# First stage by chunks with VectorE's low parts, down products one up tile later, 346 feed-forward columns

## The chip, the cores and the metric

The kernel runs on one core of one Trainium2 chip. The metric is the device time of one execution in microseconds; the kernel before took 2233.31 us (median of three runs, 2232.62 to 2235.86).

## What is computed

One inference step of a hybrid decoder layer. 1024 prompt tokens with 16 meta tokens ahead of them, and 8 single tokens of running sequences, go through a normalization, one wide projection (queries, keys, values, and the inputs and gates of a recurrent branch), attention beside the recurrence, an output projection, and then the feed-forward stage, which the change touches most. Cut to that part, for the prompt:

```python
n = rms_norm(x, g_mix)
q, k, v, xr, gr, gates = jnp.split(n @ w_in, SPLITS, axis=-1)
...
up, ffn_buf_new = causal_dwconv(rms_norm(x, g_ffn) @ w_up, ffn_buf, w_ffn_conv, b_ffn_conv)
ua, ub = jnp.split(up, 2, axis=-1)
x = x + (jax.nn.gelu(ua) * ub) @ w_down
...
y_prompt = rms_norm(xp, g_final)[:, META_TOKENS:]
```

The convolution has three taps and looks back two tokens. The model width is 1024, the inner width 2816 (each half of `up`). The rows of the 16 meta tokens are not part of `y_prompt`; their keys and values, and the last two rows of `up` for each sequence, are outputs.

## The kernel before

Activations lie with channels on the partitions and tokens along the columns: 8 decode tokens, 16 meta tokens, 1024 prompt tokens and 2 spare columns, 1050 in all, taken in three chunks of `CW` = 350. Every wide product is made of three fp32r matmuls: each operand is split into a rounded high part (an fp32r copy, made by ScalarE) and a low part (the difference, made by VectorE or GpSimd), and `project_part` (L83) issues high x high, high x low and low x high for each of the 8 blocks of 128 channels, 24 matmuls for one chunk of one 128-channel tile ("a piece").

There are five phases, each a block that all engines leave together. Within one, every engine runs its own list of instructions in the order written, and semaphores tie them together; DMAs are issued by SyncE, in order.

**`phase_qkv` (L92).** Nine token tiles (24 tokens, then eight of 128) are loaded, squared and summed by ScalarE (L279), scaled by VectorE (L343), transposed by TensorE into `a_xt` (L419), multiplied by the weight of the norm by VectorE (L356), rounded by ScalarE into `n_hi` (L298), and subtracted by GpSimd into `n_lo` (L260). Two weight tiles are rounded in between (L285) and subtracted by GpSimd (L254). TensorE waits for all nine low parts and then makes 12 pieces for keys and values (four channel tiles `j` times three chunks `c`, by `j` first), each emptied by ScalarE from one of two banks (L308) into `kv_ch`. Then it transposes these (L448), and projects the queries.

**`phase_mix`** (attention, recurrence, gates) is the longest and isn't touched. **`phase_out` (L1391)** projects, adds the residual, normalizes each token tile again (L1520 to L1539), and writes `n_hi` and `n_lo` for the next phase.

**`phase_ffn` (L1583).** The inner width is taken in 11 turns of two 128-channel pairs. A turn has four up tiles (two of each half, three pieces each, from the banks of `p_up` in alternation), each emptied by ScalarE (`up_tile`, L1720), run through the convolution by VectorE (`conv`, seven chained operations, L1787 to L1801), the first of each pair through a gelu on ScalarE (L1725), and multiplied (`gated`, L1807). The product is rounded by ScalarE (`high_a`, L1730) and subtracted by VectorE (`low_a`, L1814). The down products of a turn are 24 chunks of 6 matmuls (8 output tiles times three chunks, L1870) that VectorE adds into `y` (L1823) from four banks. They are issued during the next turn, six behind each of its four up tiles. Weights come through two raw slots of `w_raw`; ScalarE rounds them (`high_up` L1706, `high_down` L1711), GpSimd subtracts (`low_up` L1676, `low_down` L1681), and SyncE loads the next one as soon as the low part is made. The first turn's up tiles stand ahead of the loop, the last turn's down products behind it. The order written for ScalarE around a turn's boundary is:

```python
high_down(0, nth(m, DOWNC, DOWNC - 1), 1, 16 * nth(m, 3, 2))
high_down(1, nth(m, DOWNC, DOWNC - 1), 0, 16 * nth(m, 3, 3))
high_a(m, 0)
up_tile(i, 0, (0, 1))
high_a(m, 1)
high_up(1, nth(i, UPC, -1, 6), 1, 16 * nth(m, 3, 3))
up_tile(i, 0, (2,))
```

where a rounding of down weights waits for the previous turn's last down product. On TensorE it is, for `u` from 0 to 3, `up_tile(m + 1, u, ...)` and then `down(m, ..., down_part(u))`; on VectorE `add_down(m, down_part(u))`, then `conv(m + 1, u)`, and `gated` behind each second one, with `low_a(m)` ahead of it all.

**`phase_last` (L1898)** transposes `y` back, adds the residual, normalizes and stores.

## Time and profile before

| | |
|---|---|
| median of three runs | 2233.31 us |
| the profiled execution | 2233.16 us, span 2231.4 us |
| mean granted TensorE clock | 0.937 |
| TensorE matmul busy | 1941.0 us (87%), 14580 matmuls |
| VectorE / ScalarE / GpSimd busy | 1209.2 (54%) / 941.7 (42%) / 247.5 us (11%) |
| up products L87, 3 groups | 1056 matmuls of 350 columns each, 325 ns mean |
| down products L1870 in the loop, 3 groups | 480 matmuls of 350 columns each, 328 to 332 ns mean |
| loads of up weights, issue to landing | 512 KB each, 3.7 us |

A matmul's duration overlaps its neighbours', so starts and not durations give its pace. A row of a timeline gives the start in us from the span's start, the duration, engine, line, operation and tiles, and in brackets how long the engine stood idle before and whose result ended that. A GpSimd, VectorE or ScalarE row with "x2" merges two instructions that follow each other.

### The profile page before, as it was taken

The numbers are of one execution on the slowest core, as the hardware profiler recorded it, in microseconds if no ns is written. First come the engines' busy times: TensorE is split into PE (matmuls) and PEld (weight loads), VectorE is DVE, ScalarE is ACT, GpSimd is POOL, SyncE is SP. The second block draws the span as 40 slices with busy tenths as digits, with TensorE's granted clock in tenths as the row PEclk, the third lists the DMA queues.
The fourth block names the chain that finished last, engine by engine and source line by source line (L and its number), as shares of the span: only waits on it lengthen the run. The fifth ranks groups of instructions, "written<-read, shape, count | busy, mean of one in ns | idle before, by whom it ended". The sixth has DMA issues, their size and how long they took to land. (4 is left out here: it accounts for less than half of the span.)

```text
span 2231.4 us, 41433 instructions
## 1 busy us (share of the span) xinstructions
PE 1941.0 (87%) x14580; PEld 1764.3 (79%) x14580; DVE 1209.2 (54%) x2020; ACT 941.7 (42%) x1514; POOL 247.5 (11%) x117
## 2 busy tenths in 40 slices
PE   3997898979797988979797796899999999999985
PEld 3897887758585867768585586899999999999985
DVE  6100566647484756647485534555555455545555
ACT  4112577666666666666667211221221222212213
POOL 4111000000000000000001202211221122212210
PEclk9999998979898998979898898999999999999998
DMA  3242312131222222131222221101111111111104
GB/s 114 77 114 70 103 44 78 51 84 49 78 62 74 77 58 59 51 84 48 79 58 78 93 91 56 57 22 54 47 47 38 38 47 47 38 38 47 47 19 168
DMA packets 198746, 144.02 MB, mean 65 GB/s; under 512 B 58293, under 2 KB 187894, under 8 KB 198548
## 3 DMA queue, kind: packets, MB, share of 16 engines
q1 hardware_dynamic: 198574, 141.80, 21.8%
q8 instruction: 99, 1.62, 0.3%
q14 instruction: 73, 0.60, 0.1%
HBM read 124.38 MB, written 17.61 MB: 64 GB/s over the span
## 5 line engine op out<-in xcount | busy, mean ns | idle before, releaser
L87 PE MATMUL d_p_up<-n_hi,d_w_hi 128*128 128x350 f32 x1056 | 343.7, 325 | 14.0 <-POOL d_w_lo L1676 7.7
L87 PE MATMUL d_p_up<-n_lo,d_w_hi 128*128 128x350 f32 x1056 | 342.7, 325 | 0.0
L87 PE MATMUL d_p_up<-n_hi,d_w_lo 128*128 128x350 f32 x1056 | 342.5, 324 | 0.0
L1823 DVE TENSOR_TENSOR mix<-mix,d_p_down 128x350 f32<-128x350 f32 x264 | 137.2, 520 | 323.8 <-PE d_p_down L1870 323.8
L1720 ACT ACTIVATE d_up<-d_p_up 128x350 f32<-128x350 f32 x132 | 60.6, 461 | 502.3 <-PE d_p_up L87 502.3
L87 PE MATMUL b_p_proj<-n_hi,b_w_hi 128*128 128x350 f32 x768 | 268.0, 349 | 4.5 <-ACT r_gr L969 4.5
L87 PE MATMUL b_p_proj<-n_lo,b_w_hi 128*128 128x350 f32 x768 | 252.6, 329 | 0.0
L87 PE MATMUL b_p_proj<-n_hi,b_w_lo 128*128 128x350 f32 x768 | 251.9, 328 | 0.0
L87 PEld LDWEIGHTS d_p_up<-n_hi,d_w_hi 128*128 128x128 f32 x1056 | 200.6, 190 | 15.0 <-POOL d_w_lo L1676 8.1
L1072 DVE TENSOR_TENSOR_SCAN b_sums<-b_sums 128x720 f32<-128x720 f32 (+16 forms) x136 | 171.1, 1258 | 60.2 <-ACT b_sums L1006 55.1
L87 PEld LDWEIGHTS d_p_up<-n_hi,d_w_lo 128*128 128x128 f32 x1056 | 200.6, 190 | 0.0
L87 PEld LDWEIGHTS d_p_up<-n_lo,d_w_hi 128*128 128x128 f32 x1056 | 200.4, 190 | 0.0
L1233 PE MATMUL b_p_z<-b_k_in,b_q_in 64*64 64x360 f32 (+16 forms) x1024 | 101.9, 460 | 102.2 <-ACT b_z L954 46.5
L1870 PE MATMUL d_p_down<-d_a_hi,d_wd_hi 128*128 128x350 f32 x480 | 159.4, 332 | 23.8 <-DVE d_a_lo L1814 23.8
L953 ACT ACTIVATE b_sums<-b_p_z,b_bias 128x720 f32<-128x720 f32 (+16 forms) x136 | 94.8, 697 | 197.5 <-PE b_p_z L1240 145.1
L1676 POOL TENSOR_TENSOR d_w_lo<-w_raw,d_w_hi 128x1024 fp32r<-128x1024 f32 x45 | 114.2, 2549 | 522.1 <-ACT d_w_hi L1706 522.1
L1058 DVE COPY mix<-b_p_misc 128x64 f32 (+2 forms) x136 | 29.9, 220 | 248.9 <-PE b_p_misc L1271 241.1
L1870 PE MATMUL d_p_down<-d_a_hi,d_wd_lo 128*128 128x350 f32 x480 | 158.3, 330 | 0.0
L87 PEld LDWEIGHTS b_p_proj<-n_hi,b_w_hi 128*128 128x128 f32 x768 | 151.9, 198 | 7.5 <-ACT r_gr L969 6.4
L1870 PE MATMUL d_p_down<-d_a_lo,d_wd_hi 128*128 128x350 f32 x480 | 157.6, 328 | 0.0
L87 PEld LDWEIGHTS b_p_proj<-n_lo,b_w_hi 128*128 128x128 f32 x768 | 151.0, 197 | 0.0
L87 PEld LDWEIGHTS b_p_proj<-n_hi,b_w_lo 128*128 128x128 f32 x768 | 149.1, 194 | 0.0
(248 smaller groups left out, 3916.9 us busy)
## 6 DMA issues: line engine op xcount, KB each, us to landing
w_raw<-in_w_in SPq DMA_DIRECT2D x45, 512.0 KB, 4.8
w_raw<-in_w_up SPq DMA_DIRECT2D x45, 512.0 KB, 3.7
b_page<-in_cache_k SPq DMA_DIRECT2D x128, 128.0 KB, 2.1
b_page<-in_cache_v SPq DMA_DIRECT2D x128, 128.0 KB, 2.1
w_raw<-in_w_down SPq DMA_DIRECT2D x22, 512.0 KB, 3.2
b_q_in<-q_scr SPq DMA_DIRECT2D x272, 32.0 KB, 2.2
q_scr<-a_q_stage SPq DMA_DIRECT2D x16, 260.0 KB, 3.3
mix<-in_x_prompt SPq DMA_DIRECT2D x8, 512.0 KB, 7.3
```

The lines of the kernel that those rows point to most:

```text
L87: last = pe.matmul(out, w[:, k, :], x[:, k, col:col + CW], start=(k == 0 and w is w_hi and x is x_hi), stop=(k == KT - 1 and w is w_lo))
L953: own.mark(act.activation(so, pz, ACT.Abs, bias=bias[:, 0:1]))
L1058: dve.tensor_copy(g.mix[:, bass.ds(i if s >= 0 else i - 1, 1), FIRST + q0:FIRST + q0 + nq] .rearrange("p a c -> p (a c)"), p_av[:, 0:nq]). ...
L1072: dve.tensor_tensor_scan(pos[:, ::-1], so[:, ::-1], pos[:, ::-1], 0.0, ALU.add, ALU.add)\
L1233: last = pe.matmul(banks[bank][QB * a:QB * (a + 1), 0:k1 - k0], q_in[rows, Q_AT[s], a, :], k_in[rows, k0:k1], start=True, stop=k1 <= diagonal)
L1676: pool.tensor_tensor(w_lo[:, slot, :, :], w_raw[:, raw, :, :], w_hi[:, slot, :, :].bitcast(F32), ALU.subtract).then_inc(lo_ready, 1)
L1720: act.activation(up[:, u % 2, CW * c:CW * (c + 1)], p_up[:, n % 2, 0:CW], ACT.Copy).then_inc(up_out, 1)
L1823: dve.tensor_tensor(to, to, p_down[:, n % 4, 0:CW], ALU.add).then_inc(down_out, 1)
L1870: last = pe.matmul(p_down[:, n % 4, 0:CW], w[:, k, P * tile:P * (tile + 1)], a[:, k, CW * c:CW * (c + 1)], start=(k == 0 and w is wd_hi an ...
```

## The change

Five things. In the first stage the pieces are made in another order (`FIRST_PIECES`: chunk by chunk for the first two channel tiles, then tiles 2 and 3), the first two in halves between the transposes of token tiles 5 to 8; each waits only for the token tiles of its own chunk. VectorE makes the low parts of the token tiles and of the first two weights, in a loop that runs one tile behind the multiply; ScalarE squares two tiles ahead, and SyncE's order of loads follows. In the feed-forward loop no down product follows the first up tile of a turn and eight follow each of the other three; the weight of the second up tile is loaded, rounded and subtracted ahead of the two down weights, the second of which is rounded after the second chunk of the turn's first up tile is emptied. And the feed-forward stage leaves out 14 of the 16 meta tokens: the 8 decode tokens are moved to columns 14 to 21, next to the last two meta tokens that the convolution still needs, and the stage's chunks are 346 columns from column 12 on. The last stage reads the decode tokens from there and leaves out the meta tokens' rows. The convolution loses the memset that had set the columns ahead of the prompt to zero.

```diff
+FIRST_PIECES = [(j, c) for c in range(CHUNKS) for j in range(2)] + [(j, c) for j in (2, 3) for c in range(CHUNKS)]
...
                 for t in range(2, TILES):
                     load_x(t)
-                    if t == 4:
-                        load_w(0, 1, K_COL)
-                load_w(1, 2, K_COL + P)
+                    if t in (3, 5):
+                        load_w(t // 2 - 1, t // 2, K_COL + P * (t // 2 - 1))
...
-                    sp.wait_ge(proj_out, 2 + CHUNKS * (j + 1))
+                    sp.wait_ge(proj_out, 2 + FIRST_PIECES.index((j, CHUNKS - 1)) + 1)
...
-                for t in range(TILES):
-                    c0, nr = token_tile(t)
-                    pool.wait_ge(hi_ready, t + 1)
-                    pool.tensor_tensor(g.n_lo[:, :, c0:c0 + nr], tmp[:, t % 2, :, 0:nr],
-                                       g.n_hi[:, :, c0:c0 + nr].bitcast(F32), ALU.subtract).then_inc(lo_ready, 1)
-                    if t == TILES - 2:
-                        low_part(0, 1)
-                low_part(1, 2)
...
                 square(0)
+                square(1)
                 for t in range(TILES + 1):
...
-                    if t + 1 < TILES:
-                        square(t + 1)
+                    if t + 2 < TILES:
+                        square(t + 2)
...
-                    if t in (7, 9):
-                        high_part((t - 7) // 2, 3 * (t - 5) // 2, 16)
+                    if t in (5, 7):
+                        high_part((t - 5) // 2, 3 * (t - 3) // 2, 16)
+                    if t == TILES:
+                        kv_piece(0)
...
+                for p in range(2, len(FIRST_PIECES)):
+                    kv_piece(p)
+                    if p in (4, 5):
+                        high_part(p - 4, 6 + p + 1, 32)
...
+                    if t >= 2:
+                        u = t - 2
+                        c0, nr = token_tile(u)
+                        dve.wait_ge(hi_ready, u + 1)
+                        dve.tensor_tensor(g.n_lo[:, :, c0:c0 + nr], tmp[:, u % 2, :, 0:nr],
+                                          g.n_hi[:, :, c0:c0 + nr].bitcast(F32), ALU.subtract).then_inc(lo_ready, 1)
+                    if t in (5, 7):
+                        n = (t - 5) // 2
+                        dve.wait_ge(w_hi_ready, n + 1)
+                        dve.tensor_tensor(w_lo[:, n, :, :], w_raw[:, n, :, :], w_hi[:, n, :, :].bitcast(F32),
+                                          ALU.subtract).then_inc(w_lo_ready, 1)
...
+                def first_piece(p, k0, k1):
+                    j, c = FIRST_PIECES[p]
+                    if k0 == 0:
+                        pe.wait_ge(lo_ready, tiles_for_chunk(c))
+                        if c == CHUNKS - 1:
+                            pe.wait_ge(consts, 9)
+                        pe.wait_ge(w_lo_ready, j + 3)
+                        pe.wait_ge(proj_out, p + 1)
...
-                pe.wait_ge(lo_ready, TILES)
-                pe.wait_ge(consts, 9)
+                    if t in (5, 7):
+                        first_piece(t // 2 - 2, 0, KT // 2)
+                    if t in (6, 8):
+                        first_piece(t // 2 - 3, KT // 2, KT)
+                for p in range(2, 6):
+                    first_piece(p, 0, KT)
...
+FTOK = HEAD_ROWS - 2
+FDEC = FTOK - DEC
+F0 = FDEC - 2
+FW = (COLS - F0) // CHUNKS
...
-            return range(DOWNC // 4 * u, DOWNC // 4 * (u + 1))
+            return range(DOWNC // 3 * (u - 1), DOWNC // 3 * u) if u else range(0)
...
                 with sp.Fori(0, TURNS - 1, 1) as m:
-                    load_down(1, nth(m, 6, 5), m, 0)
-                    load_down(0, nth(m, 6, 6), m, 1)
-                    for n in (1, 2, 3):
+                    load_up(1, nth(m, 6, 5), m + 1, 1)
+                    load_down(0, nth(m, 6, 6), m, 0)
+                    load_down(1, nth(m, 6, 7), m, 1)
+                    for n in (2, 3):
                         load_up(n % 2, nth(m, 6, n + 6), m + 1, n)
...
-                    low_down(0, nth(m, 2, 0), 1)
-                    low_down(1, nth(m, 2, 1), 0)
-                    for n in (1, 2, 3):
+                    low_up(1, nth(m, 4, 5), 1)
+                    low_down(0, nth(m, 2, 0), 0)
+                    low_down(1, nth(m, 2, 1), 1)
+                    for n in (2, 3):
                         low_up(n % 2, nth(m, 4, n + 4), n % 2)
...
-                    high_down(0, nth(m, DOWNC, DOWNC - 1), 1, 16 * nth(m, 3, 2))
-                    high_down(1, nth(m, DOWNC, DOWNC - 1), 0, 16 * nth(m, 3, 3))
+                    high_up(1, nth(i, UPC, -1, 6), 1, 16 * nth(m, 3, 2))
+                    high_down(0, nth(m, DOWNC, DOWNC - 1), 0, 16 * nth(m, 3, 3))
                     high_a(m, 0)
-                    up_tile(i, 0, (0, 1))
+                    up_tile(i, 0, (0,))
                     high_a(m, 1)
-                    high_up(1, nth(i, UPC, -1, 6), 1, 16 * nth(m, 3, 3))
+                    up_tile(i, 0, (1,))
+                    high_down(1, nth(m, DOWNC, DOWNC - 1), 1, 16 * nth(m, 3, 3))
                     up_tile(i, 0, (2,))
...
-                        project(pe, p_up[:, n % 2, 0:CW], w_hi[:, u % 2], w_lo[:, u % 2],
-                                g.n_hi, g.n_lo, CW * c).then_inc(up_done, 1)
+                        project(pe, p_up[:, n % 2, 0:FW], w_hi[:, u % 2], w_lo[:, u % 2],
+                                g.n_hi, g.n_lo, F0 + FW * c, FW).then_inc(up_done, 1)
...
                     for u in range(4):
-                        up_tile(m + 1, u, nth(m, 6, 6 + u if u else 4, 2))
-                        down(m, nth(m, 6, 6, 2), down_part(u))
+                        up_tile(m + 1, u, nth(m, 6, (4, 5, 8, 9)[u], 2))
+                        down(m, nth(m, 6, 7, 2), down_part(u))
```

The other lines of the diff follow from the new column numbers: the bounds of the convolution, the gelu, the products and the additions, two more small memsets for the two spare columns 12 and 13, the head tile's multiply in `phase_out` in two parts (8 decode and 2 meta columns), and the head tile's rows in `phase_last`.

## Rows read from the trace of the kernel before

**Rows 1.** Busy us by engine in stretches; then granted clock, DMA share, GB/s

```profile
52.20:101.60 49.40, 48.54 (x289) 47.67 (x290) 4.82 (x18) 8.40 (x15) 9.51 (x5) 1.00 0.22 60
...
212.00:1366.00 1154.00, 971.33 (x8672) 810.52 (x8672) 692.15 (x1142) 700.49 (x1140) 27.04 (x15) 0.90 0.25 69
...
1438.90:2165.40 726.50, 692.85 (x4248) 690.03 (x4249) 394.51 (x682) 154.06 (x219) 150.29 (x60) 0.98 0.14 42
```

**Rows 2.** What TensorE waited for: total us, times, longest us

```profile
PE a_xt L419 <- DVE mix L343: 27.6, 8, 7.2
...
PE d_p_down L1870 <- DVE d_a_lo L1814: 23.8, 10, 2.5
...
PE d_p_up L87 <- ACT d_up L1720: 6.3, 2, 4.9
...
PE a_proj L87 <- POOL n_lo L260: 6.9, 1, 6.9
```

**Rows 3.** Timeline, first stage, VectorE: start, duration (us), instruction, [idle before]

```profile
12.31 0.79 DVE L343 TENSOR_SCALAR mix<-mix,a_stat 128x1024 f32<-128x1024 f32 x1
13.02 1.21 DVE L356 TENSOR_TENSOR a_tmp<-a_xt,par 128x1024 f32<-128x1024 f32 x1
...
15.64 2.48 DVE L343 TENSOR_SCALAR mix<-mix,a_stat 128x1024 f32<-128x1024 f32 x1
```

**Rows 4.** Timeline, first stage, ScalarE, GpSimd and TensorE

```profile
10.51 1.06 ACT L279 ACTIVATE a_junk<-mix 128x1024 f32<-128x1024 f32 x1 [2.98 <-DMA mix<-in_x_prompt]
...
15.40 2.18 POOL L260 TENSOR_TENSOR n_lo<-a_tmp,n_hi 128x1024 fp32r<-128x1024 f32 x1 [2.85 <-ACT n_hi L298]
...
52.27 0.66 PE L87 MATMUL a_proj<-n_hi,a_w_hi 128*128 128x350 f32 x1 [6.95 <-POOL n_lo L260]
...
101.59 1.05 PE L448 MATMUL a_xt<-ident,a_kv_ch 128*24 128x128 f32 x8 [0.55 <-ACT a_kv_ch L308]
```

**Rows 5.** Single lines' instructions, VectorE: min/median/max ns

```profile
L1539 DVE TENSOR_TENSOR n_lo<-r_rg,n_hi x9: 360/1226/1227, 1263.2 to 1361.0; 128x1024 fp32r<-128x1024 f32 x8, 128x192 fp32r<-128x192 f32 x1
...
L1038 DVE TENSOR_TENSOR b_w_lo<-w_raw,b_w_hi x33: 1215/1224/1226, 215.7 to 1178.6; 128x1024 fp32r<-128x1024 f32 x33
```

**Rows 6.** Timeline, TensorE: 55 intervals of 350 columns, 36 of 512

```profile
1501.96 0.32 PE L87 MATMUL d_p_up<-n_hi,d_w_hi 128*128 128x350 f32 x1
...
1510.80 0.32 PE L87 MATMUL d_p_up<-n_lo,d_w_hi 128*128 128x350 f32 x1
...
1301.33 0.39 PE L1548 MATMUL c_p_x<-c_wo_hi,n_lo 128*128 128x512 f32 x1
...
1309.71 0.39 PE L1548 MATMUL c_p_x<-c_wo_hi,n_lo 128*128 128x512 f32 x1
```

**Rows 7.** Timeline, feed-forward loop, TensorE: first three of ten such rows

```profile
1441.02 0.42 PE L1870 MATMUL d_p_down<-d_a_hi,d_wd_hi 128*128 128x350 f32 x1 [2.13 <-DVE d_a_lo L1814]
...
1514.70 0.42 PE L1870 MATMUL d_p_down<-d_a_hi,d_wd_hi 128*128 128x350 f32 x1 [2.46 <-DVE d_a_lo L1814]
...
1586.81 0.43 PE L1870 MATMUL d_p_down<-d_a_hi,d_wd_hi 128*128 128x350 f32 x1 [2.42 <-DVE d_a_lo L1814]
```

**Rows 8.** Busy time and granted clock, stretches of the feed-forward loop

```profile
1441.00:1446.00 5.00, 4.99 (x21) 4.99 (x22) 1.30 (x3) 0.60 (x1) 4.52 (x2) 0.66 0.30 87
...
1519.60:1583.00 63.40, 63.40 (x397) 63.40 (x396) 34.39 (x62) 12.13 (x18) 9.65 (x4) 1.00 0.14 43
```

**Rows 9.** Timeline, one turn's boundary: GpSimd, VectorE, ScalarE

```profile
1501.85 4.81 POOL L1681 TENSOR_TENSOR d_wd_lo<-w_raw,d_wd_hi 128x1024 fp32r<-128x1024 f32 x2 [20.37 <-ACT d_wd_hi L1711]
...
1501.98 4.70 DVE L1795 SCALAR_TENSOR_TENSOR d_cv<-d_fp,d_cv 128x8 f32<-128x8 f32 x2
...
1515.96 0.52 DVE L1823 TENSOR_TENSOR mix<-mix,d_p_down 128x350 f32<-128x350 f32 x1 [1.39 <-PE d_p_down L1870]
...
1511.66 1.08 ACT L1730 ACTIVATE d_a_hi<-d_prod 128x1048 fp32r<-128x1048 f32 x1 [2.77 <-DVE d_prod L1807]
```

**Rows 10.** Timeline, ScalarE, end of the loop's first boundary

```profile
1438.29 1.08 ACT L1730 ACTIVATE d_a_hi<-d_prod 128x1048 fp32r<-128x1048 f32 x1 [2.75 <-DVE d_prod L1807]
```

More of the change, by code:

```diff
@@ L86, in project_part @@
         for w, x in ((w_hi, x_hi), (w_hi, x_lo), (w_lo, x_hi)):
-            last = pe.matmul(out, w[:, k, :], x[:, k, col:col + CW],
+            last = pe.matmul(out, w[:, k, :], x[:, k, col:col + width],
                              start=(k == 0 and w is w_hi and x is x_hi), stop=(k == KT - 1 and w is w_lo))
     return last
+FIRST_PIECES = [(j, c) for c in range(CHUNKS) for j in range(2)] + [(j, c) for j in (2, 3) for c in range(CHUNKS)]
 def phase_qkv(nc, g, sem):
@@ L285, in high_part, with evacuate, kv_piece @@
                     act.activation(w_hi[:, slot, :, :], w_raw[:, slot, :, :], ACT.Copy).then_inc(w_hi_ready, 1)
+                def evacuate(bank, index, out, scale):
+                    act.wait_ge(proj_done, index + 6)
+                    act.activation(out, proj[:, bank, 0:CW], ACT.Copy, scale=scale).then_inc(proj_out, 1)
+                def kv_piece(p):
+                    j, c = FIRST_PIECES[p]
+                    evacuate(p % 2, p + 1, kv_ch[:, j, CW * c:CW * (c + 1)], 1.0)
                 square(0)
+                square(1)
                 for t in range(TILES + 1):
@@ L332, in _, with mean @@
                 own = Chain(dve, dve_step)
-                for t in range(TILES + 1):
-                    if t < TILES:
-                        _, nr = token_tile(t)
-                        dve.wait_ge(squared, t + 1)
-                        dve.tensor_scalar(stat[0:nr, 1, t:t + 1], stat[0:nr, 0, t:t + 1], 1.0 / D, EPS,
-                                          ALU.mult, ALU.add).then_inc(meaned, 1)
+                def mean(t):
+                    _, nr = token_tile(t)
+                    dve.wait_ge(squared, t + 1)
+                    dve.tensor_scalar(stat[0:nr, 1, t:t + 1], stat[0:nr, 0, t:t + 1], 1.0 / D, EPS,
+                                      ALU.mult, ALU.add).then_inc(meaned, 1)
+                mean(0)
+                for t in range(TILES + 2):
+                    if t + 1 < TILES:
+                        mean(t + 1)
                     if t < TILES:
@@ L438, in tile @@
                         last.then_inc(proj_done, 1)
-                for n in range(4):
+                for n in (2, 3):
                     tile(n % 2, n + 1, CHUNKS * n, 0)
@@ L1499, in _ @@
                     act.wait_ge(scaled, t + 1)
-                    act.activation(g.n_hi[:, :, c0:c0 + nr], tmp[:, :, 0:nr], ACT.Copy).then_inc(hi_ready, 1)
+                    r0 = 0 if t else FDEC
+                    act.activation(g.n_hi[:, :, c0 + r0:c0 + nr], tmp[:, :, r0:nr], ACT.Copy).then_inc(hi_ready, 1)
             @block.vector
@@ L1534, in _ @@
                         dve.wait_ge(lo_ready, t)
-                    dve.tensor_tensor(tmp[:, :, 0:nr], p_xt[:, :, 0:nr],
-                                      g.par[:, :, R_GFFN:R_GFFN + 1].to_broadcast([P, KT, nr]),
-                                      ALU.mult).then_inc(scaled, 1)
+                    r0 = 0 if t else FDEC
+                    for to, src, n in ((0, 0, nr),) if t else ((FDEC, 0, DEC), (FTOK, FTOK, nr - FTOK)):
+                        last = dve.tensor_tensor(tmp[:, :, to:to + n], p_xt[:, :, src:src + n],
+                                                 g.par[:, :, R_GFFN:R_GFFN + 1].to_broadcast([P, KT, n]), ALU.mult)
+                    last.then_inc(scaled, 1)
                     dve.wait_ge(hi_ready, t + 1)
-                    dve.tensor_tensor(g.n_lo[:, :, c0:c0 + nr], tmp[:, :, 0:nr],
-                                      g.n_hi[:, :, c0:c0 + nr].bitcast(F32), ALU.subtract).then_inc(lo_ready, 1)
+                    dve.tensor_tensor(g.n_lo[:, :, c0 + r0:c0 + nr], tmp[:, :, r0:nr],
+                                      g.n_hi[:, :, c0 + r0:c0 + nr].bitcast(F32), ALU.subtract).then_inc(lo_ready, 1)
             @block.tensor
@@ L1778, in _ @@
                     dve.sem_inc(s, n)
-                CONV = 7
+                CONV = 6
                 def conv(i, u):
@@ L1869, in down @@
                             for w, a in ((wd_hi, a_hi), (wd_hi, a_lo), (wd_lo, a_hi)):
-                                last = pe.matmul(p_down[:, n % 4, 0:CW], w[:, k, P * tile:P * (tile + 1)],
-                                                 a[:, k, CW * c:CW * (c + 1)],
+                                last = pe.matmul(p_down[:, n % 4, 0:FW], w[:, k, P * tile:P * (tile + 1)],
+                                                 a[:, k, F0 + FW * c:F0 + FW * (c + 1)],
                                                  start=(k == 0 and w is wd_hi and a is a_hi),
```

83 lines of the change are left out of this document (44 added, 39 removed).

## The prediction, made before the change was run

> **What bounds the kernel now.** I read the busy times by stage first [rows 1]: in the key and value projections (52.2 to 101.6 us) TensorE is busy 48.5 of 49.4 us, in the feed-forward loop 692.9 of 726.5; in the attention stage between them (1154 us), which the change doesn't touch, 84%. So an edit pays in three ways: TensorE starts sooner, waits less, or has fewer columns. The list of TensorE's waits [rows 2] shows what there is to win: 27.6 us in the first stage for scaled token tiles, ending in one of 6.9 for the last low part, and 23.8 us in the loop, ten waits for VectorE's low parts of the activations. The timelines show why. In the first stage the scaling L343 takes 0.79 us while GpSimd is idle and 2.48 while GpSimd makes a low part of 2.18 us [rows 3, 4]; with it a tile takes 5.03 us (from one scaling to the next), and TensorE holds every projection until the ninth tile is through, at 52.27 [rows 4]. In the loop the low parts come 2.1 to 2.5 us after the first up tile of a turn has ended, and the down products stand right behind that tile [rows 7].
>
> Durations are those of the profiled execution, 2233.16 us, 0.15 below the median of the runs shown.
>
> **First stage.** GpSimd loses its nine token low parts and the first two weight ones; VectorE gains them at 1.23 and 1.22 us each, the time of the same subtraction elsewhere [rows 5]. With GpSimd idle I price the scaling at 0.79 for every tile. A tile then costs VectorE 0.79 + 1.21 + 1.23 and two single-column operations of 0.15: 3.54 us. ScalarE's squares move one tile ahead, so its root for tile 1 stands behind the square of tile 2, whose data land at 10.51 [rows 4]; tile 1 is scaled at about 12.2 where today's tile 2 is (12.31): one tile is lost at the start, and won back at 1.5 per tile. Scalings at 12.2, 14.7 (a short first tile), 18.2, 21.8, 25.4. Then VectorE waits for ScalarE's rounded weights and subtracts (about 2.2 us): weight low part at 30.7, tile 6 at 31.1, tile 7 at 34.7, the second weight at 40.7, tile 8 at 40.9; today 41.75. So the tiles are hardly earlier, but nothing of 2.18 us follows them, and TensorE has two pieces done in the gaps. Those halves are also in the way: half a piece is 12 matmuls, 1.9 us at 0.161 and twice that at the lower clock, and tile 8's transposes stand behind one that starts at 41, so I let them end at 45.5. Multiply (46.7), round (47.8), empty the first piece's bank, which ScalarE does only after that: the third piece starts at 49.0. Ten pieces of 24 matmuls at 0.1607 [rows 6] are 38.6; two weight waits and the last emptying, 1.2. The transposes of keys and values start at 88.8 instead of 101.59 [rows 4], 12.8 us sooner; half a slow-clock spell of some 1.5 us (priced below) off that, at even odds, less a little rounding: **-12.3**. Bounds: -8, if the third piece starts at 52 like today's first and a spell comes on top; -14, if TensorE is at full clock throughout. SyncE now issues the first weight load ahead of token tile 4 and the second ahead of tile 6; a weight is 512 KB like a tile, so tile 4 and tiles 6 to 8 land one load later. Their squares are due from 14.5 and from 21.5 us on, and in today's run ScalarE waited for no tile after 10.51: nothing. The stores of k_scr wait for pieces 5 and 6, which now come before the third and fourth weights; the loads behind them on SyncE are due some 20 us later. Nothing else moves with this stage.
>
> **Down products one up tile later.** Let T be the end of a turn's last down product (1500.67 here: the stall of [rows 7] begins at 1512.24, one up tile of 72 x 0.1607 = 11.57 before is T). Now the activations' low parts end at T + 13.9 and are due at T + 11.6. After: due after two up tiles, T + 22.9. They also come sooner: at T GpSimd makes one down low part, not two, and the convolution's little STT L1795, held for 4.70 us by two of them [rows 9], is held by one; rounding ends near T + 9.9 and not T + 12.05, low parts at T + 11.4. All ten waits go: **-23.8** [rows 2]. What is late next: VectorE must be through conv 0 before eight additions start at T + 22.9. It gets there at about T + 21, held twice by GpSimd's parts at T + 11.4 to 16.3, and four down banks give 3 us of grace. The additions take 0.52 against 0.95 of a chunk, GpSimd running or not [rows 9]. Weight loads are each issued as soon as their raw slot is free, the tightest (tile 2's) landing some 3 us before ScalarE wants it.
>
> The stalls have a second price. Of the ten 5 us stretches behind them, five have a granted clock of 0.66 to 0.69 [rows 8]: a part at 1.2 GHz after TensorE stood for 2.4 us. All the time between is at 1.00, so with no stall the clock stays at 2.4. Turns without such a spell are 72.1 us from one stall's end to the next, with one 73.4 to 73.7 [rows 7]: 5 x 1.5 = **-7.5**.
>
> One wait is added. Bank 1 of the up products is emptied by ScalarE behind its rounding of the second activation, where today it goes before. Ready at T + 11.45 for the next tile's first chunk, emptied at T + 10.4: hidden. Not in the first turn, where GpSimd makes an up and a down part at the boundary as it makes two down parts now and the rounding ends at 1439.37 [rows 10], 0.5 after the up tile: with 0.46 for the emptying TensorE waits once, **+1.0**.
>
> **346 columns.** 350 columns start every 160.7 ns, 512 every 232.8 (8.84 us over 55, 8.38 over 36) [rows 6]: 0.445 ns a column, hardly a fixed part. Four columns are 1.78 ns, over 1056 x 3 up and 528 x 3 down matmuls. The 288 of turn 0 I leave out: VectorE and a GpSimd memset set its pace (6.3 us of TensorE's waits for emptied banks [rows 2]). 4464 x 1.78: **-7.9**. Bounds: 0, if the weight load that goes with each matmul binds just below 350; -8.2, in strict proportion.
>
> The Trainium skill, "TensorE: Matmul & The Clock Gate", section "Back-to-back issue gap", gives a sustained 81 ns at 128 columns and 131 at 512, with weights loaded each time. Its slope, 0.13 ns a column, would make this term -2.3 and the time 2188; its 131 ns stands against 232.8 here, so the rows decide. Rival (1) below holds that outcome too.
>
> **The rest.** The convolution loses 14 columns of 1040 and a memset of 0.06 us on an engine busy 54% of the loop [rows 1]; if that cover went it would be 0.1 us a tile. The head tile's multiply in the output stage becomes two small ones (+0.1 us under other tiles' products); the last stage's first tile has 8 rows for 24, while its chain waits for full tiles: 0. The final 9.8 us wait ahead of the last 24 down chunks has the same chain behind it and stays.
>
> Sum: -12.3 - 23.8 - 7.5 + 1.0 - 7.9 = -50.5 from 2233.2: **2182.7 us**.
>
> **Rivals.** (1) The columns are worth little, since the spacing hangs on something else than columns; for it only that 346 was never run, against it the line through two widths. 2185 to 2191. (2) The new wait for bank 1 comes in every turn: if conv 3 is held by two low parts as now, rounding ends at T + 12.05, emptying at T + 12.5: 1.05 us x 9 more, and a slow spell of 1.5 behind half of them, 2199. For it: the order on ScalarE; against: GpSimd's up part falls in the eight additions, which it doesn't hold. (3) The first stage wins little, because in-order halves of pieces hold back the last transposes and VectorE is now its bound: 2190 to 2195. (4) Slower: the column starts. Chunks now begin at bytes 48, 1432 and 2816, not 0, 1400 and 2800. If that made a matmul slower it would strike 4464 times; it decides from 10.6 ns each (42.6 saved elsewhere and the 4.5 us of 0.2%), 7% of 160.7; at 15 ns 2258. Against it: three starts with unlike remainders run at one spacing today, since the 55 intervals cover all three. (5) The saving isn't had at all, because the attention stage absorbs the earlier start: at its beginning TensorE waits for keys loaded only after the first stage has closed, so I see no way.
>
> **Numbers.** Forecast 0.68, (1) 0.10, (2) 0.09, (3) 0.08, (4) 0.03, (5) 0.02. The range: below, all terms at their best (-14, -31.3, -8.2) give 2179.7 and a few spells fewer in the attention stage (clock 0.90) 2177; above, (2) and (3): 2200. 0.2% is 4.5 us, about what a measurement of this kernel can tell from none. Faster 0.95, same 0.02, slower 0.03.
>
> **What would show it.** Right: the third piece near 49, the key transposes near 89; no wait of TensorE on the low activations; turns of 432 x 0.159 = 68.7 us at clock 1.00; a spacing of 158.9. Wrong: TensorE waiting on L1720 at each turn's second up tile; scalings still at 2.5 us; a spacing of 160.7 or more.

## The result, and the profile after

The changed kernel takes 2161.82 us (median of four runs, 2157.11 to 2166.46) against 2234.59 us for the kernel before, run beside it (four runs, 2232.62 to 2239.73): ratio 0.967, 95% interval 0.964 to 0.970. That is 72.8 us less where 50.5 were forecast, and the time is below the range. The profiled execution is 2160.42 us, its span 2158.7. Cut at the same instructions, the two profiled spans differ like this:

| stretch of TensorE's time | before, us | after, us | difference | forecast |
|---|---|---|---|---|
| start to the key transposes | 101.6 | 84.8 | -16.8 | -12.3 |
| key transposes to the first attention product | 120.1 | 120.2 | +0.1 | 0 |
| attention, to the first output product | 993.9 | 980.6 | -13.3 | 0 |
| output stage, to the first up product | 150.7 | 150.4 | -0.3 | 0 |
| feed-forward, to the last turn's down products | 799.1 | 756.7 | -42.4 | -38.2 |
| the rest | 66.0 | 66.0 | 0 | 0 |

Busy time by engine in stretches of the kernel after; the columns are those of [rows 1]:

```profile
45.09:84.80 39.71, 39.06 (x240) 38.48 (x240) 4.09 (x21) 9.27 (x16) 7.19 (x3) 1.00 0.21 54
205.00:1336.00 1131.00, 968.72 (x8672) 808.00 (x8672) 689.61 (x1138) 697.12 (x1134) 25.83 (x10) 0.91 0.26 70
1440.00:2083.00 643.00, 643.00 (x4050) 643.00 (x4049) 378.07 (x600) 142.98 (x205) 140.36 (x57) 1.00 0.15 45
```

In the feed-forward loop TensorE is now busy all the time, at full clock (2.4 GHz). In the attention stage it has the same number of matmuls as before, and almost the same busy time (968.7 against 971.3 in [rows 1]); by the table the stage is 13.3 us shorter all the same, so it was waits that went. (The two stretches are not cut alike: the one in [rows 1] begins 9.7 us ahead of the first attention product.)

What TensorE waited for in the kernel after (total us, times, longest), to be set beside [rows 2]:

```profile
PE a_xt L450 <- DVE mix L349: 14.0, 5, 9.4
PE b_p_z L1268 <- issue: 10.8, 3, 4.0
...
PE d_p_up L87 <- ACT d_up L1765: 6.8, 3, 4.8
```

The waits for low activations (23.8 us) and for the last low part (6.9 us) are gone, those for scaled tiles halved. The second row is of the attention stage, and the change has no line there. Its row in the kernel before:

```profile
PE b_p_z L1233 <- issue: 18.9, 3, 6.6
```

The first stage after, VectorE, ScalarE, TensorE; the rows answer to [rows 3, 4]:

```profile
9.84 0.75 DVE L349 TENSOR_SCALAR mix<-mix,a_stat 128x1024 f32<-128x1024 f32 x1
...
16.41 0.75 DVE L349 TENSOR_SCALAR mix<-mix,a_stat 128x1024 f32<-128x1024 f32 x1
17.08 1.22 DVE L362 TENSOR_TENSOR a_tmp<-a_xt,par 128x1024 f32<-128x1024 f32 x1
18.21 1.22 DVE L369 TENSOR_TENSOR n_lo<-a_tmp,n_hi 128x1024 fp32r<-128x1024 f32 x1
...
19.71 0.75 DVE L349 TENSOR_SCALAR mix<-mix,a_stat 128x1024 f32<-128x1024 f32 x1
...
37.63 0.75 DVE L349 TENSOR_SCALAR mix<-mix,a_stat 128x1024 f32<-128x1024 f32 x1
...
42.28 1.22 DVE L362 TENSOR_TENSOR a_tmp<-a_xt,par 128x1024 f32<-128x1024 f32 x1 [1.63 <-PE a_xt L450]
...
8.37 1.06 ACT L273 ACTIVATE a_junk<-mix 128x1024 f32<-128x1024 f32 x1
...
13.84 1.06 ACT L273 ACTIVATE a_junk<-mix 128x1024 f32<-128x1024 f32 x1 [0.96 <-DMA mix<-in_x_prompt]
...
45.09 0.40 PE L87 MATMUL a_proj<-n_hi,a_w_hi 128*128 128x350 f32 x1 [0.92 <-ACT a_kv_ch L283]
...
84.82 1.05 PE L483 MATMUL a_xt<-ident,a_kv_ch 128*24 128x128 f32 x8 [0.55 <-ACT a_kv_ch L283]
```

No scaling is held any more (0.75 us for 2.48), a tile comes every 3.30 us (16.41 to 19.71) for 5.03, and the third piece starts at 45.09.

The feed-forward loop after, TensorE; the first of these rows is the only wait that the change adds to this stage, the next two are the first down products of two turns, the last is the wait ahead of the last turn's:

```profile
1408.36 0.42 PE L87 MATMUL d_p_up<-n_hi,d_w_hi 128*128 128x346 f32 x1 [0.64 <-ACT d_up L1765]
...
1488.56 0.32 PE L1917 MATMUL d_p_down<-d_a_hi,d_wd_hi 128*128 128x346 f32 x1
...
1557.19 0.32 PE L1917 MATMUL d_p_down<-d_a_hi,d_wd_hi 128*128 128x346 f32 x1
...
2092.73 0.63 PE L1917 MATMUL d_p_down<-d_a_hi,d_w_hi 128*128 128x346 f32 x1 [9.26 <-issue]
```

Where [rows 7] have 2.1 to 2.5 us of idle time in front of the turn's down products there is none, and a turn takes 68.63 us, 432 matmuls at 158.9 ns.

So the parts that were forecast came, a little larger; the 13.3 us in a stage whose code is the same are the surprise. There the two traces part at the jump from the end of the attention loop back to its head, on TensorE. The jump into the fourth turn, before:

```profile
574.99 0.18 PEld L1233 LDWEIGHTS b_p_z<-b_k_in,b_q_in 64*64 64x64 f32 x1 [3.67 <-issue]
...
578.19 0.30 PEld L1233 LDWEIGHTS b_p_z<-b_k_in,b_q_in 64*64 64x64 f32 x7 [3.02 <-issue]
578.19 1.48 PE L1233 MATMUL b_p_z<-b_k_in,b_q_in 64*64 64x360 f32 x8 [6.42 <-issue]
```

and after:

```profile
555.45 0.34 PEld L1268 LDWEIGHTS b_p_z<-b_k_in,b_q_in 64*64 64x64 f32 x8 [3.79 <-issue]
555.48 1.48 PE L1268 MATMUL b_p_z<-b_k_in,b_q_in 64*64 64x360 f32 x8 [3.37 <-issue]
```

Before, TensorE stands 3.67 us, loads one weight tile, and stands another 3.02 us before the other seven. After, it stands once and all eight follow. "issue" means that it waited for no semaphore or transfer that the profile shows. The first of the eight turns stands ahead of the loop, so the loop jumps back six times. The jumps into the sixth and the eighth turn show the same pair (4.07 and 2.83, 3.60 and 2.61 us). At those into the third, fifth and seventh TensorE waits for the keys behind the jump, in both kernels: from the start of the jump to the second weight load it is 7.5 to 7.7 us before and 7.4 to 8.1 after, so nothing is won there.

The jump instruction has records of its own. In the kernel before, that of the attention loop and that of the feed-forward loop (min/median/max in ns; the last of each goes on without a jump and is the shortest):

```profile
L1378 PEldq COMPARE_BRANCH  x7: 83/3478/3719, 445.9 to 1196.2; - x7
...
L1890 PEldq COMPARE_BRANCH  x10: 76/208/231, 1497.7 to 2152.6; - x10
```

A jump of the attention loop takes 3.3 to 3.7 us (3.6 to 4.1 in the kernel after), one of the feed-forward loop 0.2.

The theory that I took from this: the engine fetches its instructions in blocks. The loop has 2184 TensorE instructions, counted in the compiled program; its first was number 3032 of the engine's program and is now number 3037, because the new first stage has five more waits. If a block's edge lies just behind number 3032, the jump fetches one block, runs a few instructions, and waits for the next; five further on, the whole head lies in one block. The number alone doesn't show this (3032 is 40 short of a multiple of 256): the pair of waits does, and only shifting the loop can test it. The Trainium skill, "Runtime: NRT & Kernel Launch", section "Instruction fetch mechanics", says that instructions are refilled in blocks of 256, that TensorE holds 2048 (a later line of it has a window of two blocks), and that a taken branch to an instruction that isn't present has to fetch the target's block before it goes on. The page has no time for it; the traces give 3.3 to 4.1 us for the first block and 2.5 to 3.2 for a second. The rivals: the 13 us belong to another part of the change (an earlier start of the attention stage falls better among its loads), or they are scatter between profiles.

### The profile page after: what moved, and what is told of

Read it like the earlier page. It is cut to its first block and busy times, and to the rows that moved or that the text cites. A ratio compares the mean times of both kernels' runs of the same rounds, so it can differ in the third digit from the quotient of the medians.

```text
span 2158.7 us, 41137 instructions
## 1 busy us (share of the span) xinstructions
PE 1917.7 (89%) x14580; PEld 1744.8 (81%) x14580; DVE 1215.5 (56%) x1990; ACT 940.2 (44%) x1514; POOL 222.7 (10%) x106
## 5 line engine op out<-in xcount | busy, mean ns | idle before, releaser
L87 PE MATMUL d_p_up<-n_hi,d_w_hi 128*128 128x346 f32 x1056 | 341.9, 324 | 14.5 <-POOL d_w_lo L1720 7.7
L87 PE MATMUL d_p_up<-n_hi,d_w_lo 128*128 128x346 f32 x1056 | 341.3, 323 | 0.0
L87 PE MATMUL d_p_up<-n_lo,d_w_hi 128*128 128x346 f32 x1056 | 341.1, 323 | 0.0
L1868 DVE TENSOR_TENSOR mix<-mix,d_p_down 128x346 f32<-128x346 f32 x264 | 136.3, 516 | 267.6 <-PE d_p_down L1917 267.6
L1765 ACT ACTIVATE d_up<-d_p_up 128x346 f32<-128x346 f32 x132 | 60.1, 457 | 399.7 <-PE d_p_up L87 399.7
L1720 POOL TENSOR_TENSOR d_w_lo<-w_raw,d_w_hi 128x1024 fp32r<-128x1024 f32 x45 | 109.1, 2425 | 556.2 <-ACT d_w_hi L1751 556.2
L1917 PE MATMUL d_p_down<-d_a_lo,d_wd_hi 128*128 128x346 f32 x480 | 153.8, 320 | 0.0
L1917 PE MATMUL d_p_down<-d_a_hi,d_wd_hi 128*128 128x346 f32 x480 | 153.8, 320 | 0.0
L1917 PE MATMUL d_p_down<-d_a_hi,d_wd_lo 128*128 128x346 f32 x480 | 153.7, 320 | 0.0
```

What stands on the lines that cost most here:

```text
L87: last = pe.matmul(out, w[:, k, :], x[:, k, col:col + width], start=(k == 0 and w is w_hi and x is x_hi), stop=(k == KT - 1 and w is w_lo))
L1720: pool.tensor_tensor(w_lo[:, slot, :, :], w_raw[:, raw, :, :], w_hi[:, slot, :, :].bitcast(F32), ALU.subtract).then_inc(lo_ready, 1)
L1765: act.activation(up[:, u % 2, F0 + FW * c:F0 + FW * (c + 1)], p_up[:, n % 2, 0:FW], ACT.Copy).then_inc(up_out, 1)
L1868: dve.tensor_tensor(to, to, p_down[:, n % 4, 0:FW], ALU.add).then_inc(down_out, 1)
L1917: last = pe.matmul(p_down[:, n % 4, 0:FW], w[:, k, P * tile:P * (tile + 1)], a[:, k, F0 + FW * c:F0 + FW * (c + 1)], start=(k == 0 and w i ...
```

## The experiments

### The loop's place, by itself

**Five instructions more in the kernel before**, nothing else (two waits go on one instruction):

```diff
                 pe.sem_inc(proj_done, 6)
-                pe.wait_ge(consts, 3)
+                for _ in range(12):
+                    pe.wait_ge(consts, 3)
```

> The kernel before with five more TensorE instructions at its very start, waits that are long satisfied when TensorE reaches them; the program of the attention loop then begins at the same instruction number as in the changed kernel. Theory A (code position: at each turn of the attention loop TensorE jumps back and waits for its instructions to be loaded, and five instructions more or less decide whether it waits once or twice): TensorE's wait with no visible releaser at the turn boundaries falls from about 6.4 to 3.5 us and the attention stage from 994 to about 981 us, so 10 to 13 us faster than the kernel before, about 2221. Rival B (the stage is shorter because it starts 17 us earlier or because VectorE's or ScalarE's work ahead of it differs): no change, within 3 us of the kernel before.

Measured: 2221.34 us (2215.40 to 2226.82) against 2234.74 for the kernel before beside it; ratio 0.993 (0.990 to 0.996), -13.4 us. TensorE's "issue" waits at this line fall from 18.9 to 10.9 us, with the eight loads in one group:

```profile
PE b_p_z L1234 <- issue: 10.9, 3, 3.8
```

An earlier start isn't needed: here the key transposes stand at 101.3.

**Five instructions fewer in the kernel after**, by leaving out waits that an earlier one covers:

```diff
-                        pe.wait_ge(lo_ready, tiles_for_chunk(c))
-                        if c == CHUNKS - 1:
+                        if j == 0:
+                            pe.wait_ge(lo_ready, tiles_for_chunk(c))
+                        if c == CHUNKS - 1 and j == 0:
                             pe.wait_ge(consts, 9)
-                        pe.wait_ge(w_lo_ready, j + 3)
-                        pe.wait_ge(proj_out, p + 1)
+                        if c == 0:
+                            pe.wait_ge(w_lo_ready, j + 3)
+                        if p >= 2:
+                            pe.wait_ge(proj_out, p + 1)
```

> The changed kernel without five TensorE instructions in the first stage, all waits that an earlier wait of the same engine makes superfluous; the attention loop begins at the same instruction number as in the kernel before. Theory A (code position): the double wait at the turn boundaries comes back, 10 to 13 us slower than the changed kernel, about 2173. Rival B: within 3 us of the changed kernel, 2162.

Measured: 2174.40 us (2172.36 to 2176.28), ratio 0.973 (0.971 to 0.975) to the kernel before, 12.6 us above the kernel after. The pair of waits is back:

```profile
PE b_p_z L1271 <- issue: 19.4, 3, 6.8
```

Less work for the engine, and a slower kernel.

**128 and 256 instructions more in the kernel before.** If it is blocks, then the loop's head may go anywhere in a block but not just ahead of its edge, and 256 further on it must be as bad as it was:

```diff
+                    if t < TILES - 1:
+                        for _ in range(32):
+                            pe.wait_ge(consts, 3)
                     pe.wait_ge(normed, t + 1)
```

with 64 in place of 32 for the second.

> The kernel before with 128 more TensorE instructions (256 satisfied waits, two to an instruction) spread over the idle time ahead of the first eight token transposes; the attention loop's first instruction is number 3160 instead of 3032. Theory A (the loop's jump waits for one block of instructions more when its first instruction lies just ahead of a block's edge, and blocks hold 256): the loop now begins in the middle of a block, each jump shows one wait of 3.4 to 4 us on TensorE with the eight weight loads in one group, and the time is about 13 us below the kernel before, 2221 us, plus what the waits cost the first stage (between 0 and 3 us). Rival B (five instructions moved something else, for instance which copies of the instructions are resident at the loop's end, and the distance does not matter in blocks): no gain of that size, 2233 us or slower, and the pair of waits of 3.6 and 3.0 us stays.

> The same with 256 more TensorE instructions (512 satisfied waits), so that the loop's first instruction is number 3288, exactly 256 behind where it was. Theory A (blocks of 256): the loop begins at the same place of a block as before, the pair of waits of 3.6 to 4.1 and 2.6 to 3.0 us is back at the third, fifth and seventh jump, one weight load ahead of the gap and seven behind it, and the time is that of the kernel before, 2233 us, plus what the waits cost the first stage (between 0 and 6 us). Rival B (any shift away from the old place helps, or the gain grows with the distance): about 2220 us, with one wait to a jump.

Measured beside a kernel before of 2231.15 us: 2214.29 (2212.33 to 2218.12) with 128 more, ratio 0.993 (0.990 to 0.995); 2233.81 (2228.65 to 2239.20) with 256 more, ratio 1.001 (0.9995 to 1.002). The jump into the fourth turn with 128 more, TensorE's weight loads:

```profile
570.63 0.33 PEld L1236 LDWEIGHTS b_p_z<-b_k_in,b_q_in 64*64 64x64 f32 x8 [3.71 <-issue]
```

and with 256 more:

```profile
573.51 0.13 PEld L1236 LDWEIGHTS b_p_z<-b_k_in,b_q_in 64*64 64x64 f32 x1 [3.89 <-issue]
...
576.17 0.30 PEld L1236 LDWEIGHTS b_p_z<-b_k_in,b_q_in 64*64 64x64 f32 x7 [2.54 <-issue]
```

One weight load ahead of the gap, as at the old place. So the effect repeats after 256 instructions, the block that the Trainium skill names there, and the rival that any shift would do is out. (Of the 16.9 us that 128 more give, 3.0 are in the feed-forward stage of its profile, which has two spells of the lower clock fewer.) Scatter between profiles is large: over all of this study the attention stage takes 991 to 998 us with the head at the old place of a block (five kernels, mean 994.6) and 976 to 993 us elsewhere (seven, mean 983.9). The ranges meet, so a single pair of profiles would not carry this; the four timed runs do, and the pair of waits, which stands in all five of the first kind and in none of the seven.

What isn't settled is where all of the 13 us are: the three pairs account for 8 (18.9 less 10.8), the other three jumps for nothing, and for some 5 no record tells where they are. The feed-forward loop has 909 instructions, and its jumps show no such wait: all 643.00 us of the stretch from 1440 are busy. That is more than two blocks, so of the two sizes that this section of the Trainium skill gives the trace goes with 2048. Where between 909 and 2184 the wait begins no run here shows.

### The parts of the change, one at a time

**The first stage alone**: the kernel before with `phase_qkv` of the kernel after.

> The kernel before with the first stage of the change alone (which brings its five TensorE instructions). If the parts add up, key transposes start near 84.8 instead of 101.6 us (-16.8) and, by theory A, the attention stage gives 10 to 13 more: about 2206. By rival B with the earlier start as the cause the same; by rival B with the feed-forward edits as the cause only -16.8: about 2217.

Measured: 2207.97 us (2203.53 to 2210.08), ratio 0.987 (0.985 to 0.989), -26.8. This part brings its own five instructions, so it holds the 13.4 us of the loop's place; 13.4 are left, and in its profile the key transposes come at 85.7, 15.9 us sooner. With the run with five more, half of what this edit gives is had in a stage that it doesn't touch. ScalarE, VectorE and TensorE:

```profile
10.61 1.06 ACT L273 ACTIVATE a_junk<-mix 128x1024 f32<-128x1024 f32 x1 [2.68 <-DMA mix<-in_x_prompt]
...
12.08 0.75 DVE L349 TENSOR_SCALAR mix<-mix,a_stat 128x1024 f32<-128x1024 f32 x1
...
38.53 0.75 DVE L349 TENSOR_SCALAR mix<-mix,a_stat 128x1024 f32<-128x1024 f32 x1
...
45.99 0.40 PE L87 MATMUL a_proj<-n_hi,a_w_hi 128*128 128x350 f32 x1 [0.93 <-ACT a_kv_ch L283]
```

Here tile 2 lands as late as in [rows 4], tile 1 is scaled at 12.08 as forecast (12.2), and the third piece is still only 0.90 us later than in the kernel after.

**The down products one up tile later, alone**, at 350 columns:

```diff
-            return range(DOWNC // 4 * u, DOWNC // 4 * (u + 1))
+            return range(DOWNC // 3 * (u - 1), DOWNC // 3 * u) if u else range(0)
...
-                        up_tile(m + 1, u, nth(m, 6, 6 + u if u else 4, 2))
-                        down(m, nth(m, 6, 6, 2), down_part(u))
+                        up_tile(m + 1, u, nth(m, 6, (4, 5, 8, 9)[u], 2))
+                        down(m, nth(m, 6, 7, 2), down_part(u))
```

with the order of SyncE, GpSimd and ScalarE that goes with it.

> The kernel before with the down products one up tile later alone, chunks still of 350 columns. The ten waits (23.8 us), their five slow-clock spells (7.5), the restarts behind them (about 2.8) and half a microsecond at the end go, one wait of 0.6 comes: about -34, at 2200. If clock spells come without a wait too, they stay: -26. The attention stage stays at 994 us, since nothing ahead of it changes.

Measured: 2201.97 us (2200.70 to 2205.92), ratio 0.986 (0.984 to 0.987), -32.8; the feed-forward stage of its profile is 32.4 us shorter. The loop, busy time as above, and the first down products of its first two turns:

```profile
1452.00:2123.00 671.00, 671.00 (x4172) 671.00 (x4172) 393.91 (x656) 146.51 (x209) 142.82 (x58) 1.00 0.14 44
```

```profile
1451.33 0.32 PE L1873 MATMUL d_p_down<-d_a_hi,d_wd_hi 128*128 128x350 f32 x1
...
1520.83 0.32 PE L1873 MATMUL d_p_down<-d_a_hi,d_wd_hi 128*128 128x350 f32 x1
```

No wait, full clock, and a turn of 69.50 us where the kernel before has 72.10 without a spell of the lower clock: 2.60 less for a stall listed with 2.42 [rows 7]. A stall costs 0.18 us more than its idle time, 1.8 over ten.

**346 columns alone.**

> The kernel before with the 346 columns alone (14 meta tokens left out of the feed-forward stage); first stage and order of the down products as before. Theory (0.445 ns a column): matmuls start every 158.9 ns where they started every 160.7, about -8, at 2226; the ten waits for the low activations stay at 2.4 us, the attention stage at 994. Rival (the spacing hangs on the weight load): no change beyond a microsecond. Rival (the new column starts cost time): slower.

Measured: 2220.92 us (2219.24 to 2223.66), ratio 0.994 (0.992 to 0.997), -12.8; in its profile the feed-forward stage is 11.3 us shorter. The ten stalls are still there (23.1 us), but of the 5 us behind each only three have the lower clock, where the kernel before has five [rows 8]; the three and one of the others:

```profile
1442.30:1447.30 5.00, 4.93 (x21) 4.93 (x22) 1.27 (x3) 0.68 (x1) 4.59 (x2) 0.66 0.27 79
1515.30:1520.30 5.00, 4.93 (x22) 4.94 (x23) 1.45 (x3) 0.34 (x1) 4.58 (x2) 0.69 0.28 81
1588.10:1593.10 5.00, 4.96 (x31) 4.96 (x32) 2.06 (x4) 0.35 (x1) 4.58 (x2) 1.00 0.29 84
...
1945.20:1950.20 5.00, 4.93 (x22) 4.94 (x23) 1.38 (x3) 0.39 (x1) 4.59 (x2) 0.67 0.30 88
```

Some 30 matmuls run in 5 us at full clock and 21 or 22 with a spell. Two spells of 1.5 us fewer make 3.0 of the 11.3, the ten shorter waits 0.7, the wait ahead of the last turn's down products 0.6; that leaves about 7 for the columns, and what is above 11.3 in the timed run is not assigned. The number of spells is not the columns' doing: with the turns unchanged there are five in the kernel before and three with 128 instructions more. Two turns without a spell end at these rows:

```profile
1659.58 0.42 PE L1879 MATMUL d_p_down<-d_a_hi,d_wd_hi 128*128 128x346 f32 x1 [2.32 <-DVE d_a_lo L1821]
...
1731.01 0.42 PE L1879 MATMUL d_p_down<-d_a_hi,d_wd_hi 128*128 128x346 f32 x1 [2.32 <-DVE d_a_lo L1821]
```

A turn is 71.43 us for 72.10, and 0.1 of that is the shorter stall: 1.3 ns a matmul (432 to a turn). The kernel after beside the down products alone, neither of which stalls, has 68.63 for 69.50 us: 2.0 ns. The mean over all starts of the loop that no stall and no spell disturbs says nearly the same: 160.8 ns before, 159.4 with the columns alone; 160.9 with the down products later, 158.9 with both. So some 0.6 ns of the 2.0, 2.7 us over the 4464 matmuls, come only with the two edits together, and no run shows why.

The three parts add up to 26.8 + 32.8 + 12.8 = 72.4 of the 72.8 us, in part by chance: two spells (3.0) are in both of the last two, and the 2.7 us that need both edits are in neither.

### Details of the first stage

**The old order of loads**, in the kernel after:

```diff
-                    if t in (3, 5):
-                        load_w(t // 2 - 1, t // 2, K_COL + P * (t // 2 - 1))
+                    if t == 4:
+                        load_w(0, 1, K_COL)
+                load_w(1, 2, K_COL + P)
```

> The changed kernel with the old order of loads in the first stage (first weight behind token tile 4, second behind tile 8). If the load of tile 2 lands sooner in the changed kernel because a weight and no longer a third token tile shares the DMA engines with it, ScalarE waits for tile 2 until about 10.5 us again, the chain of scalings starts near 12.2 as predicted, and the key transposes come some 2 us later (near 87 instead of 84.8); 0 to 2.5 us slower than the changed kernel. If it lands sooner for another reason, no difference at tile 2.

Measured: 2159.50 us (2155.97 to 2165.59), ratio 0.968 (0.966 to 0.971): no difference. ScalarE's squares of tiles 2 and 4, and TensorE's third piece:

```profile
9.12 1.06 ACT L274 ACTIVATE a_junk<-mix 128x1024 f32<-128x1024 f32 x1 [1.23 <-DMA mix<-in_x_prompt]
...
12.55 1.04 ACT L274 ACTIVATE a_junk<-mix 128x1024 f32<-128x1024 f32 x1
...
44.65 0.40 PE L87 MATMUL a_proj<-n_hi,a_w_hi 128*128 128x350 f32 x1 [0.93 <-ACT a_kv_ch L284]
```

The square of tile 4, which waits 0.96 us in the kernel after (13.84), doesn't wait here. That of tile 2, whose load is the same in both, waits here and not there, and the third piece is 0.44 us earlier. A load of weights among the tiles costs less than their landing differs from one profile to the next.

**The token low parts back on GpSimd**, the rest as in the kernel after:

```diff
+                for t in range(TILES):
+                    c0, nr = token_tile(t)
+                    pool.wait_ge(hi_ready, t + 1)
+                    pool.tensor_tensor(g.n_lo[:, :, c0:c0 + nr], tmp[:, t % 2, :, 0:nr],
+                                       g.n_hi[:, :, c0:c0 + nr].bitcast(F32), ALU.subtract).then_inc(lo_ready, 1)
...
-                    if t >= 2:
-                        u = t - 2
-                        c0, nr = token_tile(u)
-                        dve.wait_ge(hi_ready, u + 1)
-                        dve.tensor_tensor(g.n_lo[:, :, c0:c0 + nr], tmp[:, u % 2, :, 0:nr],
-                                          g.n_hi[:, :, c0:c0 + nr].bitcast(F32), ALU.subtract).then_inc(lo_ready, 1)
```

> The changed kernel with the nine token low parts back on GpSimd (VectorE keeps the two weight ones). Theory (one engine holds the other up): the scalings take 2.48 us again instead of 0.75 and a tile 5.0 us instead of 3.3, so the third piece starts some 7 to 10 us later than 45.1 and the whole is 7 to 10 us slower than the changed kernel, about 2170. Rival (the gain of the first stage is in the order of pieces alone, which doesn't need the last tiles until late): under 3 us slower.

Measured: 2172.95 us (2169.07 to 2181.21), ratio 0.973 (0.970 to 0.975), 11.1 us above the kernel after. GpSimd, VectorE and TensorE:

```profile
16.59 2.18 POOL L262 TENSOR_TENSOR n_lo<-a_tmp,n_hi 128x1024 fp32r<-128x1024 f32 x1 [2.85 <-ACT n_hi L306]
...
16.84 2.48 DVE L354 TENSOR_SCALAR mix<-mix,a_stat 128x1024 f32<-128x1024 f32 x1
...
53.76 0.40 PE L87 MATMUL a_proj<-n_hi,a_w_hi 128*128 128x350 f32 x1 [0.91 <-ACT a_kv_ch L288]
```

The scaling begins 0.25 us into GpSimd's subtraction and ends 0.55 behind it, as in [rows 3, 4]. The third piece comes 8.7 us later. So it is by giving work to the busier engine that the stage is freed; without that the key transposes come at 93.5, and 8.1 of the stage's 16.8 us are left.

### A version that beats both

In both kernels GpSimd sets `y` to zero in the feed-forward stage's first turn, behind the low part of the third weight, and VectorE's first copy of the convolution runs into it. One weight earlier nothing runs beside it:

```diff
-                    if n == 2:
+                    if n == 1:
                         pool.memset(y[:, 0:KT, :], 0.0).then_inc(inits, 1)
```

> The changed kernel with GpSimd's memset of the down sums (7.1 us) put one low part earlier, into 12 us in which GpSimd is idle. It now holds up VectorE's first copy of the convolution by 7.4 us, and TensorE waits 4.8 us for the bank behind it. Theory: that wait goes, 4 to 6 us faster than the changed kernel, about 2157. Rival (the convolution's own length or the parameters set the pace): under 2 us.

Measured: 2154.25 us (2151.44 to 2158.07), ratio 0.964 (0.962 to 0.967), 7.6 below the kernel after, whose runs it overlaps by 1 us; that it is faster shows in the stage: 750.2 us in its profile, 756.7 to 757.1 in the four profiles with the memset at the old place. GpSimd, VectorE, and the 5 us behind the following wait of TensorE, in the kernel after:

```profile
1353.00 7.10 POOL L1731 MEMSET mix<- 128x8400 f32 x1
...
1352.72 7.41 DVE L1833 COPY d_fp<-d_fpar 128x20 f32<-128x20 f32 x1
...
1366.10:1371.10 5.00, 4.98 (x21) 4.98 (x22) 0.00 (x0) 0.32 (x1) 0.00 (x0) 0.66 0.01 3
```

and with the memset earlier:

```profile
1342.66 7.11 POOL L1731 MEMSET mix<- 128x8400 f32 x1
...
1357.16 0.34 DVE L1833 COPY d_fp<-d_fpar 128x20 f32<-128x20 f32 x1
...
1370.00:1375.00 5.00, 5.00 (x33) 5.00 (x32) 4.70 (x8) 1.51 (x3) 2.49 (x1) 1.00 0.01 4
```

A copy of 20 columns took 7.41 us beside the memset and takes 0.34. TensorE's wait of 4.79 us for the emptied bank is gone, and with it the spell of the lower clock: 4.8 + 1.5 of the 6.5 us by which this stage is shorter.

## Why the prediction was wrong, point by point

**The step that failed** is the one that said of the attention stage that "the change doesn't touch" it and priced it at nothing, with "nothing else moves with this stage" behind the first stage. No edit lies there, but five new TensorE instructions ahead of its loop moved the loop, and its jumps cost 13 us less. The sign was luck: the kernel before had its loop at a bad place, and a change that moves it onto one loses as much, as the run with five fewer shows. The row that could have told it was in the trace of before, "b_p_z <- issue", 18.9 us in three waits, and I passed over it as belonging to a stage that stays. In the range, the lower end took all terms at their best and "a few spells fewer in the attention stage", some 3 us; what was outside is this for the most part. Without these 13 us the time would be near 2175, still just under the lower end of 2177, because the first and the feed-forward stage each gave some 4 us more than their terms, as follows.

**First stage, -12.3 forecast, -16.8 measured: mechanism right, size off.** The third piece was to start at 49.0 and starts at 45.09; from there to the key transposes it is 39.73 us for 39.8 forecast. Three things make the 3.9, and the run with the first stage alone separates them. Tile 1 is scaled at 9.84, not 12.2, because tile 2 lands earlier: I took one profile's 10.51 for a fixed time, but with the same loads ahead of it the profiles of this study have anything from 8.4 to 10.6. That is 0.9. Where tile 2 is late, tile 1 is where I put it, and tile 8 is scaled at 38.53, not 40.9: a tile costs 3.30 us, not 3.54. I added durations, but VectorE's operations begin some 0.08 us before the listed end of the one ahead (17.08 + 1.22 is 18.30, the next starts at 18.21). With the two weight parts that makes 2.3. And from tile 8's scaling to the third piece it is 7.46 us, not 8.1. The half pieces do hold back the last tile's transposes, as the forecast had it: from tile 8's scaling to their end it is 4.65 us (37.63 to 42.28) for 4.6, and VectorE stands 1.63 us there. The stage wins its time all the same, so rival (3) is out; the load order cost nothing, as said, within half a microsecond.

**Down products later, -23.8 - 7.5 + 1.0 forecast, -32.4 measured alone.** All ten waits went, the clock stays at full speed, and the one new wait came where it was put, with 0.64 us; rival (2), the wait in every turn, is out. What was missing is that a stall costs 0.18 us beyond its listed idle time, 1.8 in all.

**346 columns, -7.9 forecast, about -9.0 measured.** 2.0 ns a matmul and not 1.78, times 4464, beside the new order of the down products; with the old one it is 1.3 to 1.4, about 6. Strict proportion, the prediction's bound (-8.2), is 1.84: the one lies above it and the other below the forecast. The sum took a column's worth to be the same in either order, and it isn't; why is open. Rival (1) and the slope of 0.13 ns a column (0.5 for four) are out, so is rival (4): the new chunk starts cost nothing. "The final 9.8 us wait stays": it is 9.26, 0.6 less.

In the feed-forward stage that makes -23.8 - 1.8 - 7.5 + 0.6 - 9.0 - 0.6 = -42.1 of the -42.4.

**Rival (5)**, that the attention stage absorbs the earlier start, is out as well: from the key transposes to the first attention product it is 120.2 us for 120.1.

## What to carry to other kernels

A stage without an edit is not a stage without a change: where a loop's body is too long for the engine to hold (2184 instructions here; 909 were not), its time hangs on the place of its head, and that moves with every instruction ahead of it; so cut the two traces into stages first, and look at the jump if one without an edit differs. When a change is judged by trying its parts, pad the loop's head back to its old place, or 13 us of luck are put down to the edit. And a wait costs more than its listed idle time: the restart, and where the clock falls, that spell.

## What the runs showed of the hardware

- A jump to the head of a loop of 2184 TensorE instructions takes 3.3 to 4.1 us with no semaphore behind it; at one place of the head there is a second wait of 2.5 to 3.2 behind it. The second is gone 5 and 128 instructions further on and back at 256. A jump in a loop of 909 takes 0.2 us.
- The lower clock (granted 0.66 to 0.70 in 5 us) follows only some of ten stalls of 2.1 to 2.5 us: five in the kernel before, three with 346 columns, three also with 128 instructions more and turns as long as before.
- GpSimd's write-only memset holds a VectorE copy as long as it runs (7.41 us for 0.34), like its subtractions hold a scaling (2.48 for 0.75).
- Four columns fewer in each fp32r matmul bring the starts 1.4 ns closer in one order of the matmuls (160.8 to 159.4 ns) and 2.0 in another (160.9 to 158.9).
